# Convolutions dealt over attention steps, opening differences on VectorE, narrow weight chunks two to a place, two expert loads in halves

## The reference

```python
def _short_conv(x, w):                      # 5 taps, for q, k and v
    return lax.conv_general_dilated(x, w[:, None, :], window_strides=(1,), padding=[(2, 2)], ...)
...
gc = jnp.cumsum(g.reshape(bsz, nh, n, c), axis=-1)
decay = jnp.exp(jnp.where(incl, gc[..., :, None] - gc[..., None, :], -jnp.inf))
lmat = jnp.where(strict, jnp.einsum('bhnid,bhnjd->bhnij', kb, k) * decay, 0.0)
...
q = _apply_rope(q, cos, sin); k = _apply_rope(k, cos, sin)
p = jax.nn.softmax(jnp.einsum(...q, k), axis=-1); y = jnp.einsum(...p, v)
...
x = x + merged @ w_out[l]
x = x + _hier_moe(_rmsnorm(x, ffn_norm_w[l]), ...)   # silu(x w1[e]) * (x w3[e])) w2[e], 32 experts
```

## Time and profile before

| What | Value |
|---|---|
| Three runs | 1607.84, 1612.89 and 1615.69 us, median 1612.89 us |
| Profiled execution | 1610.73 us, of which span 1608.9 us |
| PE busy | 1302.8 us (81%) |
| DVE busy | 663.6 us (41%) |
| ACT busy | 467.2 us (29%) |
| POOL busy | 120.2 us (7%) |
| Granted clock of PE | 0.96 of full speed on average |

### The profile page before, as it was taken

The page is one execution under the profiler, slowest core; times in us unless marked ns, Lnnn a source line. Parts: engine busy times, 40 slices in busy tenths (PEclk is TensorE's granted clock), DMA queues, the critical chain, the costliest instruction groups (busy, mean ns, idle before and its releaser), DMA issues. The chain is left out here.

```text
span 1608.9 us, 46302 instructions
## 1 busy us (share of the span) xinstructions
PE 1302.8 (81%) x19436; PEld 991.5 (62%) x19437; DVE 663.6 (41%) x1598; ACT 467.2 (29%) x968; POOL 120.2 (7%) x108
## 2 busy tenths in 40 slices
PE   7998899987787676667789979999878776676665
PEld 6887687765555454445578877777555554454444
DVE  6666856662222111112285767666522221111112
ACT  4456755441111100100145566554411111100101
POOL 2002630000000000000010035200000000000000
PEclk9999999999999999999999999999999999999997
DMA  9531135499999999999954310445999999999996
GB/s 343 200 121 53 14 110 197 165 372 412 424 426 429 427 429 429 428 428 429 408 211 158 106 56 2 157 174 214 375 399 413 426 429 428 428 429 428 429 428 265
DMA packets 76747, 490.60 MB, mean 305 GB/s; under 512 B 12878, under 2 KB 15462, under 8 KB 52070
## 3 DMA queue, kind: packets, MB, share of 16 engines
q1 hardware_dynamic: 76646, 489.16, 74.7%
HBM read 488.09 MB, written 1.05 MB: 304 GB/s over the span
## 5 line engine op out<-in xcount | busy, mean ns | idle before, releaser
L2029 PE MATMUL ps<-ring,arena 128*32 128x128 f32 x5632 | 194.7, 296 | 85.2 <-DMA ring<-in_expert_w_gate_dram 72.8
L2029 PEld LDWEIGHTS ps<-ring,arena 128*32 128x32 f32 x5632 | 172.2, 119 | 115.7 <-DMA ring<-in_expert_w_gate_dram 76.1
L2109 ACT ACTIVATE arena<-ps 128x128 f32<-128x128 f32 x66 | 18.3, 277 | 525.0 <-PE ps L2029 525.0
L2258 DVE TENSOR_SCALAR arena<-cst,arena 128x128 f32 x132 | 39.8, 344 | 231.4 <-issue 225.9
L2029 PE MATMUL ps<-arena 128*32 128x128 f32 x2688 | 91.6, 292 | 38.4 <-DMA arena<-in_expert_w_gate_dram 32.6
L468 POOL TENSOR_TENSOR small<-small,cst 128x8 f32<-128x8 f32 (+1 forms) x21 | 27.5, 1309 | 1230.9 <-DVE small L718 457.6
L2029 PEld LDWEIGHTS ps<-arena 128*32 128x32 f32 x2688 | 80.7, 118 | 52.9 <-DMA arena<-in_expert_w_gate_dram 38.3
L1995 PE MATMUL ps<-xn,arena 128*32 128x256 f32 x1088 | 73.9, 389 | 42.5 <-DVE arena L2204 41.7
L1786 DVE TENSOR_TENSOR w_low<-ring,w_high 128x512 fp32r<-128x512 f32 x126 | 85.7, 705 | 51.9 <-ACT w_high L1710 51.9
L2051 PE MATMUL ps<-ring,arena 128*32 128x256 f32 x1440 | 89.0, 387 | 12.7 <-DMA ring<-in_expert_w_down_dram 12.6
L1710 ACT ACTIVATE w_high<-ring 128x512 fp32r<-128x512 f32 x126 | 77.2, 634 | 74.3 <-PE ps L1646 62.0
(11 more groups left out here) (373 smaller groups left out, 2495.3 us busy)
## 6 DMA issues: line engine op xcount, KB each, us to landing
ring<-in_expert_w_up_dram SPq DMA_DIRECT2D x44, 2048.0 KB, 39.7
ring<-in_expert_w_down_dram SPq DMA_DIRECT2D x44, 2048.0 KB, 40.5
ring<-in_expert_w_gate_dram SPq DMA_DIRECT2D x42, 2048.0 KB, 40.2
ring<-in_w_in_dram SPq DMA_DIRECT2D x28, 2048.0 KB, 7.9
arena<-in_expert_w_up_dram SPq DMA_DIRECT2D x20, 2048.0 KB, 41.5
arena<-in_expert_w_gate_dram SPq DMA_DIRECT2D x20, 2048.0 KB, 40.3
arena<-in_expert_w_down_dram SPq DMA_DIRECT2D x20, 2048.0 KB, 42.0
ring<-in_w_out_dram SPq DMA_DIRECT2D x4, 2048.0 KB, 8.3
```

Source lines behind the costliest of these rows:

```text
L2029: ins = pe.matmul(bank_b[32 * g:32 * g + 32, u * P:(u + 1) * P], xg[:, c], spare[:, c, g] if from_tenth else w[:, u, c, g], start=(c == 0) ...
L2258: v.tensor_scalar(selw[:, t], bcast(cst[:, bass.ds(r * CAP + K_IOTA, CAP)].unsqueeze(1), [P, 4, CAP]), posn[:, t, bass.ds(e, 1)], weight[: ...
```

## The change

Five edits, the same in both layers.

1. **Projection.** The eight narrow chunks share places 2 to 5 of `b_w_hi`, two to a place (`place_of`, `high_b`), and ACT waits only for the chunk whose place it takes (`held_by`). `rope(0)` and `rope(1)` move behind the low parts of chunks 15 and 16. `heads(0)` and `heads(1)` move on PE behind chunk 17, the squares of items 0 and 1 on ACT to chunk 16.
2. **Attention.** The convolutions of the values (part 2) are dealt out: the first half in step 2 with `weigh(4)` between its taps, the second half one tap at a time over steps 3 to 5. `l2scale` and `l2norm(1)` move by a place. `weigh(4)` and `weigh(5)` wait for the weights of two steps before and no longer for their y.
3. **Delta.** All sixteen differences are made by DVE; ACT is left with the four exponentials. DVE waits for two of POOL's four fills before the first level, and for the rest later.
4. **Tenth slot.** It is loaded by two transfers of 1 MB: the half that lies in `hT` right behind the load before it, the half that lies in `x_sb` where the whole stood.
5. **Down matrix of set 1** (slot 5). Each load is two transfers of 1 MB with a semaphore each; PE waits for the second one before its third quarter (c = 2).

```diff
@@ projection @@
+    NARROW = streamed_b.index(U_CKV) * KC
+    def place_of(q):
+        if NARROW <= q < NARROW + KC:
+            return 2 + (q - NARROW) // 2, 256 * (q % 2)
+        return (q if q < NARROW else q - NARROW - KC) % 6, 0
+    def high_b(q):
+        n, at = place_of(q)
+        return b_w_hi[:, n, at:at + chunks_b[q][2]]
+    def held_by(q):
+        return max((p for p in range(q) if place_of(p)[0] == place_of(q)[0] and (chunks_b[p][2] == 512 or place_of(p) == place_of(q) or chunks_b[q][2] == 512)),
+                   default=None)
...
-            if c == KC - 1 and n >= 1:
+            if q == NARROW + KC + 1:
+                for t in range(NT):
+                    heads(t)
+            if c == KC - 1 and n >= 2:
                 for t in range(NT):
                     heads(2 * (n - 1) + t)
...
-            if q >= 6:
-                act.wait_ge(b_used, q - 5)
+            if held_by(q) is not None:
+                act.wait_ge(b_used, held_by(q) + 1)
...
-            if n >= 1 and c in (3, 6):
+            if q in (NARROW + KC - 1, NARROW + KC):
+                rope(q - NARROW - KC + 1)
+            if n >= 2 and c in (3, 6):
                 rope(2 * (n - 1) + c // 6)
@@ attention @@
-                    if s >= 2:
+                    if s in (4, 5):
+                        v.wait_ge(c_prob, s - 1)
+                    elif s >= 2:
                         v.wait_ge(c_y, s - 1)
...
-                work = {0: [(convolve, 0, 0), (convolve, 0, 1)], 1: [(convolve, 1, 0), (convolve, 1, 1)], 2: [(l2norm, 0)],
-                        3: [(convolve, 2, 0, range(3))], 4: [(convolve, 2, 1, range(3))], 5: [(l2norm, 1)]}
+                work = {0: [(convolve, 0, 0), (convolve, 0, 1)], 1: [(convolve, 1, 0), (convolve, 1, 1)], 2: [(l2norm, 0), (convolve, 2, 0, range(3)), (weigh, 4), (convolve, 2, 0, range(3, TAPS))],
+                        3: [(l2scale, 0)], 4: [(convolve, 2, 1, (1,))], 5: [(convolve, 2, 1, (3,))], 6: [(l2scale, 1)]}
...
-                work_after = {6: [(decay_sums,)], 2: [(l2scale, 0)], 3: [(convolve, 2, 0, range(3, TAPS))], 4: [(convolve, 2, 1, range(3, TAPS))], 5: [(l2scale, 1)]}
+                work_after = {3: [(convolve, 2, 1, (0,))], 4: [(convolve, 2, 1, (2,))], 5: [(convolve, 2, 1, (4,)), (l2norm, 1)], 6: [(decay_sums,)]}
...
-                    if s + 1 < STEPS:
+                    if s + 1 < STEPS and s != 3:
                         weigh(s + 1)
@@ delta @@
-                            pe.wait_ge(e_d_act, 2)
+                            pe.wait_ge(e_d, 4)
...
-                def above(G):
...
+                for G in range(4):
+                    decays(G)
...
-                for G in range(2):
+                for G in range(4):
                     v.wait_ge(e_gr, G + 1)
...
-                v.wait_ge(e_m, 4)
+                v.wait_ge(e_m, 2)
...
+                v.wait_ge(e_m, 4)
                 for n in range(1, LEVELS + 1):
@@ expert loads @@
+        if n == HALVED:
+            sp.dma_start(dst[:, :, 0:2], src[:, :, 0:2]).then_inc(m_land[n], 16)
+            sp.dma_start(dst[:, :, 2:4], src[:, :, 2:4]).then_inc(m_land_half, 16)
...
+                sp.wait_ge(h_used, 2 * KC)
+                load_tenth(sp, l, 1)
                 sp.wait_ge(h_xn, NT)
                 sp.wait_ge(h_kept, 1)
-                load_expert(sp, l, SETS, 3 * SETS)
+                load_tenth(sp, l, 0)
...
+                        if c == 2 and 3 * k + 2 == HALVED:
+                            pe.wait_ge(m_land_half, landing)
```

More of the change, by code:

```diff
@@ L619, in project_scalar @@
                 w_high(q)
+            if q == NARROW + KC:
+                for t in range(NT):
+                    squares_of(t)
             if c == 3:
                 for t in range(NT):
[L623 to L624 removed]
+                    if n == 2:
+                        squares_of(2 + t)
                 for t in range(NT):
```

41 lines of the change are left out of this document (17 added, 24 removed).

## The result

The changed kernel takes 1598.56 us (median of 4 runs, 1596.73 to 1601.57), the kernel before 1614.29 us (median of 4, 1607.84 to 1616.72): ratio 0.9922, 95% interval 0.9905 to 0.9939, some 12.6 us (0.78%) faster. The ratio on record is not that of the two medians, which stand 15.7 us apart (0.9903), a little outside the interval.

What follows compares the result with a forecast made beforehand. Expert stages were taken as bound by full DMA queues, earlier stages by chains between engines. The terms, 1.15 + 3.5 + 8.2 + 1.6 + 1.0 + 0.65 = 16.1 us, gave 1596 us; range 1588 to 1606, of the sum alone 1591 to 1601.

Steps and rivals of the forecast that it cites:

- Term A: Projection: PE's stands for low parts and its half clock shrink; 1.15 us in layer 0, 3.5 us in layer 1.
- Term B: Attention: convolutions moved into DVE's idle time shorten the waits for maxima; 4.1 us per layer, 8.2 us in all.
- the parts behind are PE's and ACT's and run as before: Attention, layer 1: work behind PE's turn at 949.31 is unchanged, so the last copy of y comes 4.1 us earlier.
- Term C: Delta: eight more differences on DVE fill its stand of 2.13 us; 0.8 us per layer, 1.6 us in all.
- the size of POOL's share: Delta, first level: one product already took 1.42 us beside POOL's subtraction; the gain was put at 0.8 us per layer.
- this case: Delta: the first products, started earlier, would meet POOL's masks at the shared port and lose 1.0 us per layer.
- Terms D and E: Expert stage, layer 0: tenth slot's half queued earlier 1.0 us, slot 5 in halves 0.65 us; layer 1: 0.
- The rival of slower transfers: Expert stage: each of 24 more transfers costs 0.97 us, 23 us in all, giving 1619 us; chance 0.05.

Runs made afterwards that it cites:

- e7_masks: Changed kernel with GpSimd masking the delta's decays fully only for groups 0 and 1, output wrong; ratio 0.9892 to the kernel before.
- e3_delta: Kernel before with the delta block's part of the change alone; ratio 0.9985 to the kernel before.
- e4_tenth: Kernel before with the tenth slot loaded in halves alone; ratio 0.9984 to the kernel before.

## Why the prediction was right, and where its terms were off

The time lay 2.6 us over the forecast and well in the range. The gain was further off: 16.1 us forecast, 12.6 measured by the ratio. Some of the nearness of the time is luck, and the terms were less right than their sum. The range was not what the text calls it either: the bounds given for the terms add up to some 1585 to 1611 us, and 1591 to 1601 does not follow from them.

- **Term A, 4.65 us forecast, 4.2 measured**, as the difference of means over eight profiles with and six without the edit (1.7 and 2.5 us). The mechanism is as forecast: of the stand of 2.90 us 0.51 are left, where I had 1.0, and the low level behind it is gone. The shares of the layers were off, 1.15 and 3.5 forecast. Layer 1's 3.5 held the stand and the low clock of one profile; half of the profiles of the old order had neither in that size, and against those the edit is worth 1.1 us.
- **Term B, 8.2 us forecast, 3.83 per layer or 7.7 at the full clock.** `maxima(5)` is 1.4 us earlier (1.3 forecast), the last exponentials 3.75 (3.8), the turn of (7, 0) 4.3 (4.4). The prediction calls that one, at 949.31, PE's last turn; the last is (7, 1), and it came 2.7 us earlier. The step that failed is the next, that "the parts behind are PE's and ACT's and run as before": PE may run at its low level behind the stands that remain, 1.87, 1.54 and 0.76 us, and that is now in the chain. In the first pair of profiles it left 0.59 and 2.70 us. Over all blocks without added matmuls, each with the clock that it got, the means are 83.5 and 83.8 us in the old order, 80.2 and 80.4 in the new: 3.3 and 3.4 us. So the clock takes 0.4 to 0.5 us per block of the edit's 3.83 on average, and the first pair, whose old blocks were the shortest two of ten, made it look like far more.
- **Term C, 1.6 us forecast, 0 measured** (-0.17 and 0.13 in the pair, 0.15 per layer alone, 0.2 by the length of the opening). DVE's stand was filled and the products came earlier, as forecast; the step that failed is the size of POOL's share. I knew of one slow product and left it 0.8 us of gain; two products and the copies are slow now. I had put down 1.0 us more for this case, and that is near what happened: 1.32 and 1.00 us in place of 0.43, and 1.8 us of the opening back where two masks are left out. By the Trainium skill, "SBUF — State Buffer", section "Who interferes with whom", the shared port is an exclusive lock, and the later of two such readers is blocked. The trace agrees: the first product ends 0.3 us after the masks (956.38 against 956.09).
- **Terms D and E, 1.65 us forecast, 1.4 measured in layer 0**: six kernels with both edits took 500.4 us on average, five with neither 501.8 (e7_masks is left out, since its experts' jobs are others). In layer 1 the same kernels took 514.3 and 513.2, with 511.6 to 515.7 for single ones: no gain, as forecast, and no loss that can be told from chance. The 1.4 us are known to about 1 us, as single profiles differ by 2. The 3.2 us in layer 0 of the first pair were in part the clock and the long profile of before.
- **The rival of slower transfers** was rightly held small: 0.19 us each at the most, against the 0.67 from which it would have decided. The Trainium skill's fixed 2.0 us ("DMA: Bandwidth & Descriptors", section "Anatomy of one DMA — SWDGE (gpsimd) path") is a fit to transfers issued from GpSimd, and these are issued by SyncE; for 24 transfers it would be 48 us (an estimate by that page) if nothing hid it. The traces show 427 GB/s with halves and 428 without, so next to none of it shows in the backlogged stage.

The terms as measured, with the clock that the attention blocks got (3.3 + 3.4), are 4.2 + 6.7 + 0 + 1.4 = 12.3 us, against 12.6 by the ratio. The terms are known to about 1 us each, so part of that nearness is chance. The ratios of the parts alone give 3.7 + 7.1 + 2.4 + 2.6 - 1.1 = 14.7 us, each known to about 2 us.

Open is where e3_delta and e4_tenth got ratios of 0.9985 and 0.9984 from, more than their blocks show; intervals of 2 us leave room for chance. Open too is which stand brings a low piece of the clock, and why one execution has it here and the next there: the runs show only that filled stands keep them away where none is left over.

## What to carry to other kernels

When idle time is taken out of a chain, ask what the next engine does in the stands that are left: in the first pair of profiles a quarter to nearly all of a gain of 3.8 us per block was gone to TensorE's low clock behind stands of 1 to 2 us (over all profiles an eighth), and 15 matmuls that nobody reads, sized to fit just into the stands, kept the clock full. Work that moves to an idle engine, or to an earlier time, has neighbours: look at what another engine reads in the stretch in which it will run, since here two products took two to three times as long beside GpSimd and the whole gain was gone. And before one profile serves as the base of a sum, compare its untouched stages with those of other executions: here they differed by 2 to 4 us, as much as most of the terms. A better ruler than the length of a stage is a distance that the clock did not change: the opening of the delta block, up to PE's first level, was 14.7 us long in all eight blocks of the changed kernel's order, while the blocks themselves had 64.4 to 65.7.

## What was not expected of the hardware

- The low level of TensorE's clock comes in pieces of 3.4 us, none to four per attention block, at other places in each execution of the same order of instructions. The new order takes 78.26 us with none, 79.7 to 79.9 with one, 81.5 with two, 82.7 with four.
- A matmul of float32 with 128 columns of the identity took 0.235 us as two records, where a transpose of the same size took 0.13 (eight in 1.03 us) at the same full clock.
- Equal stages of different kernels differed by more than I had thought: layer 0's projection 78.6 to 80.7 us with the same edit, layer 1's expert stage 511.6 to 515.1 us where neither of its edits was in.
- Layer 1's projection in the old order took 72.6 to 73.6 us or 70.6 to 70.9, as PE ran low behind its stand or some 8 us before it.
